# Two reordered edits and one merged instruction in a two-block transformer kernel on one NeuronCore

## The reference, cut to what matters

```
g = sigmoid(gates + gate_bias)                                # three gates of 1024 columns a token
mixed = g[0] * (ya @ w_oa) + g[1] * (yb @ w_ob) + g[2] * (yc @ w_oc)     # the output projections
x = x + mixed @ w_out
x = x + memory_cross_attention(rmsnorm(x), rmsnorm(mem), w_mq, w_mkv, ..., w_mo)
```

## Time and profile before

| | |
|---|---|
| runs | 1175.42 us median of 3 |
| profiled execution | 1174.49 us, span 1172.8 us |
| PE busy | 1143.1 us (97%) |
| DVE busy | 811.8 us (69%) |
| ACT busy | 621.8 us (53%) |
| mean granted TensorE clock | 0.996 |
| DMA | 164 GB/s read over the span; a 1 MB load of `w_up` lands in 5.8 us |

### The profile page before, as it was taken

How to read it: one execution, slowest core, us unless ns; L and a number is a source line. 1 busy time by engine, 2 the same in 40 slices (tenths; PEclk the granted TensorE clock), 3 DMA queues, 4 the chain that set the end, 5 groups by cost and what they waited for, 6 DMA issues and landing times.

```text
span 1172.8 us, 16767 instructions
## 1 busy us (share of the span) xinstructions
PE 1143.1 (97%) x6741; PEld 997.6 (85%) x6741; DVE 811.8 (69%) x884; ACT 621.8 (53%) x808; POOL 81.7 (7%) x114
## 2 busy tenths in 40 slices
PE   8999999899999999999999999999999998999997
PEld 8978888798987799999888888888777887888886
DVE  6897657866878577777548777547866747777743
ACT  7666446436578455555445444436356547444432
POOL 7101100200000000000000000002700000000000
PEclk9999999999999999999999999999999999999999
DMA  8644333324665344645655656565634533666560
GB/s 259 194 153 144 102 108 108 121 96 146 229 199 181 108 162 145 215 155 205 216 179 179 197 181 197 187 205 167 203 117 135 180 108 125 192 204 182 181 212 36
DMA packets 143396, 193.95 MB, mean 165 GB/s; under 512 B 6168, under 2 KB 119192, under 8 KB 143320
## 3 DMA queue, kind: packets, MB, share of 16 engines
q1 hardware_dynamic: 142120, 188.43, 49.6%
q0 software_dynamic: 1200, 4.46, 1.1%
HBM read 191.82 MB, written 1.05 MB: 164 GB/s over the span
## 4 chain that ended last, share of the span: by engine, by line
PE 82%; DVE 10%; ACT 4%; issue 2%; DMA 1%; SPq 0%; DVEq 0%; ACTq 0%
PE banks L1342 22%; PE banks L1376 20%; PE banks L1324 13%; PE banks L1345 11%; PE banks L1361 5%; DVE wlo L1948 4%; PE banks L1352 2%; PE banks L1602 1%; ACT whi L1662 1%; PE banks L1487 1%; PE banks L1390 1%; PE banks L1474 1%; DMA raw<-in_w_in 1%; PE banks L1560 1%; PE banks L1432 0%
## 5 line engine op out<-in xcount | busy, mean ns | idle before, releaser
L1948 DVE TENSOR_TENSOR wlo<-raw,whi 128x2048 fp32r<-128x2048 f32 (+1 forms) x178 | 406.4, 2291 | 124.2 <-ACT whi L1662 124.1
L1662 ACT ACTIVATE whi<-raw 128x2048 fp32r<-128x2048 f32 (+1 forms) x179 | 340.1, 1903 | 246.0 <-PE banks L1345 142.9
L1342 PE MATMUL banks<-xhl,whi 128*128 128x512 f32 x1200 | 384.6, 402 | 2.9 <-DVE y5l L2291 1.8
L1345 PEld LDWEIGHTS banks<-xhl,wlo 128*128 128x128 f32 x1200 | 225.4, 188 | 53.2
L1345 PE MATMUL banks<-xhl,wlo 128*128 128x256 f32 x1200 | 236.3, 278 | 0.0
L1342 PEld LDWEIGHTS banks<-xhl,whi 128*128 128x128 f32 x1200 | 183.9, 189 | 9.5 <-issue 4.6
L1324 PE MATMUL banks<-xhl,whi 128*128 128x256 f32 x912 | 165.5, 284 | 1.1 <-DVE wlo L1948 0.5
L1324 PEld LDWEIGHTS banks<-xhl,whi 128*128 128x128 f32 x912 | 142.0, 192 | 1.9 <-DVE xhl L1975 1.0
L1324 PE MATMUL banks<-xhl,wlo 128*128 128x256 f32 x456 | 129.0, 283 | 0.0
L1376 PE MATMUL banks<-whi,hh 128*128 128x512 f32 x264 | 102.9, 390 | 0.0
L1376 PE MATMUL banks<-wlo,hh 128*128 128x512 f32 x264 | 102.8, 389 | 0.0
(11 more groups left out here) (374 smaller groups left out, 1542.6 us busy)
## 6 DMA issues: line engine op xcount, KB each, us to landing
raw<-in_w_in SPq DMA_DIRECT2D x40, 1024.0 KB, 5.3
raw<-in_w_up SPq DMA_DIRECT2D x22, 1024.0 KB, 5.8
raw<-in_ffn_w_gate SPq DMA_DIRECT2D x22, 1024.0 KB, 5.4
raw<-in_ffn_w_up SPq DMA_DIRECT2D x22, 1024.0 KB, 5.3
raw<-in_ffn_w_down SPq DMA_DIRECT2D x22, 1024.0 KB, 5.0
raw<-in_w_down SPq DMA_DIRECT2D x11, 1024.0 KB, 5.4
raw<-in_w_out SPq DMA_DIRECT2D x8, 1024.0 KB, 5.2
raw<-in_xa_wkv SPq DMA_DIRECT2D x8, 1024.0 KB, 5.5
```

The lines of the kernel that those rows point to most:

```text
L1342: pe.matmul(bank(b[m]), wh[:, k, m * P:(m + 1) * P], both[:, k, :, :].rearrange("p a t -> p (a t)"), start=(k == 0), stop=(k == KD - 1), s ...
L1345: ins = pe.matmul(bank(b[m])[:, 0:T], wl[:, k, m * P:(m + 1) * P], Xh[:, k, :], start=False, stop=(k == KD - 1), skip_group_check=True)
L1662: act.activation(columns(whi, c, part), columns(raw, c, part), ACT.Copy).then_inc(act_done, 1)
L1948: dve.tensor_tensor(columns(wlo, c, part), columns(raw, c, part), columns(whi, c, part), ALU.subtract).then_inc(dve_done, 1)
```

## The change

Three edits. The output projections exchange their bank pairs: i = 0 writes (2, 3), i = 1 writes (0, 1). `g_vb` becomes one `tensor_tensor` over 128 x 512 with beta broadcast along each head's 128 columns, in place of four `tensor_scalar` over 128 x 128. For memory attention alone, the links are cut in another place: lane 0 becomes [sc0 sm0 ex0] [pn0] [pt0 sc2 pc0] [pv0 oc0 ol0 sm2 ex2] [pn2] [pt2 pc2] [pv2 oc2 ol2], and lane 1 likewise. With it, when `mm` has to force links because a step that it needs isn't placed, only chains that still contain such a step are forced; the others are taken if they fit.

```diff
-                            i=i, banks=(2 * i, 2 * i + 1), evac="gated"))
+                            i=i, banks=(2 - 2 * i, 3 - 2 * i), evac="gated"))
...
-    def hook(force=False):
-
-        chosen = [chain for chain in side if chain and (force or fits(chain))]
+    def hook(force=False, until=()):
+
+        chosen = [chain for chain in side if chain and (force or fits(chain) or any(s[1:] in until for link_ in chain for s in link_ if not callable(s)))]
...
         while any(step not in pl.number for step in pl.ready[c]) and side:
-            hook(True)
+            hook(until=[step for step in pl.ready[c] if step not in pl.number])
...
-            if nxt is not None:
+            if nxt is not None and kind in ("mem",):
+                turn_.insert(1, ("pe", "sc", kind, nxt))
+                out_ += [("dve", "sm", kind, nxt), ("act", "ex", kind, nxt)]
+            elif nxt is not None:
                 turn_ = [turn_[0], ("pe", "sc", kind, nxt), turn_[1], ("dve", "sm", kind, nxt), ("act", "ex", kind, nxt)]
                 out_.insert(1, ("dve", "pn", kind, nxt))
             links += [turn_, out_]
+            if nxt is not None and kind in ("mem",):
+                links += [[("dve", "pn", kind, nxt)]]
...
-                for h in range(NH):
-                    ins = dve.tensor_scalar(gVb[:, h, :], bank(5)[:, h * P:(h + 1) * P], gcols[:, t, 0, h:h + 1], None, ALU.mult)
-                ins.then_inc(dve_done, 1)
+                dve.tensor_tensor(gVb[:, :, :], per_head(bank(5)), gcols[:, t, 0, :].unsqueeze(2).to_broadcast([P, NH, P]),
+                                  ALU.mult).then_inc(dve_done, 1)
```

## The result

The changed kernel took 1178.05 us in the median of 7 runs (1176.52 to 1179.02); the kernel before took 1173.95 us beside it (1173.04 to 1175.80). The ratio is 1.0029, with a 95% interval of 1.0017 to 1.0040, some 3.4 us, which is how far the means lie apart (1177.9 and 1174.5); the medians lie 4.1 us apart. Measured a second time the ratio was 1.0026 (1.0016 to 1.0036; medians 1178.06 and 1174.54). So the change makes the kernel slower, by about 0.3%. The forecast was +1.7 us, 1177.1 us. The profiled execution after took 1177.11 us with a span of 1175.4, against 1174.49 and 1172.8: +2.6 us.

A forecast was written before the change was run, and what follows sets the result against it. The prediction took the kernel as a PE stream, busy 97% of the span, with a few gaps. Its terms, -0.84 - 0.43 + 2.95 = +1.7 us, gave 1177.1 us on the median, range 1173.6 to 1179.6.

The forecast's parts named there:

- Part A: Output projection banks: chunk 33 starts 1.47 us sooner, chunk 35 then waits 0.6 us for `gated 33`; -0.84 us kept.
- Part B: Second `g_vb` before `l_u`: one instruction of 687 ns replaces four taking 1.12 us; -0.43 us carried on.
- 0, if that wait grew: Bound on the `g_vb` gain: nothing saved if PE's following 0.88 us wait for ACT's `z_x` grew.
- Part C: Memory attention: `hi 52` behind `ex2` delays chunk 51 by 0.55 us and chunk 52 by 2.95; cost +2.95 us.
- Whether the clock falls during chunk 51 does not matter here: Before chunk 52: PE would be through by 407 either way, and DVE's row sets the end.
- The sum: Whole kernel: -0.84 - 0.43 + 2.95 = +1.7 us, put on the median as 1177.1 us.
- A second fall of the clock: Rival, gaps around `pt3` and `pv3`: clock falls again, costing 1.5 us; total +3.2, 1178.6 us; chance 0.33.
- the main case: Whole kernel: the three edits' terms add to +1.7 us, 1177.1 us, range 1176.2 to 1178.2; chance 0.40.
- The outputs do come early: Rival at chunk 51: `ol1` ends before `pv1`, removing the 2.22 us wait and clock fall; -5.0, 1170.4 us; chance 0.13.
- Part C does nothing: Rival in chunk 51: `pn3` keeps its place, `pt3` and `pv3` stay hidden; -1.3 us, 1174.1 us; chance 0.14.
- adds up for slower: Whole kernel above 1177.8 us: second fall but for a sixth, plus a fifth of the main case; chance 0.37.
- equal gaps need not cost the same: PE clock: the monitor runs on its own phase, so a thin stretch around 406.9 to 410.8 us is at risk.

The follow-up runs named there:

- part C alone: Only the memory attention links and `until` changed, banks and value scaling as in the kernel before; ratio 1.0037 against that kernel.
- e9: The changed kernel itself, all three edits, measured a second time against the kernel before; ratio 1.0026, median 1178.06 us.
- e6: All three edits, and the planner may place a memory attention link 1.0 us ahead of its inputs instead of 0.5; ratio 0.9987 against the kernel before.
- B alone: Only the `g_vb` value scaling made one DVE instruction instead of four, against the kernel before; ratio 0.9998.
- e1: Only the bank pairs of the two output projections swapped, against the kernel before; ratio 0.9996.
- e7: Bank swap and single `g_vb`, old memory attention links, planner allowed 1.0 us ahead of inputs; ratio 0.9984 against the kernel before.
- e8: Bank swap and single `g_vb`, old memory attention links, planner allowed 2.0 us ahead of inputs; ratio 1.0009 against the kernel before.
- e11: Bank swap and single `g_vb`, old links, plus 12 unread transposes filling PE's wait ahead of chunk 51; ratio 0.9987 against the kernel before.
- e4: Bank swap and single `g_vb` together, memory attention as in the kernel before; ratio 0.9988 against that kernel.
- e10: Changed kernel with unread transposes filling PE's waits ahead of chunk 51, `pt3`, `pv3` and chunk 52; ratio 1.0018 against the kernel before, median 1176.14 us.
- e12: Bank swap and single `g_vb`, old links, planner allowed 1.0 us ahead, no transposes, measured again; ratio 0.9983 against the kernel before.

## Why the prediction came out as it did

**Part A: right.** -0.84 forecast, -0.72 kept when alone, and the wait that takes back a part is the one named, 0.71 us for `gated 33` against 0.6 worked out.

**Part B: the size of the step right, the term wrong.** "So each call becomes 0.43 us shorter" holds to 0.01 us, and the 0.88 us wait did not grow, as forecast. What failed is that the gain is carried to the end: of 0.43 some 0.31 to 0.36 is lost at the `hn_mul` of `mk1`, in every profile with part B. The bound "0, if that wait grew" was near the end of it, by another wait than the one named.

**Part C: the mechanism right, the size near.** The order of the three lists is the one worked, step for step, and 2.95 us became 2.7 (2.71 in the first profile of the change, 2.66 in the second, 2.69 alone). "Whether the clock falls during chunk 51 does not matter here" is nearly right. With a fall the two chunks start 11.8 us apart in both profiles of the change, and 11.3 where the clock was held by filling. With part C alone the spacing was 11.8 again without that fall; there the fall at 408.6 us made `pv3` longer (1.60 us against 1.13). In all three the 0.5 us is paid. What the sum left out is the other side: with the old order the fall at 400 us costs the full 1.6 us. Where it did not come (the banks alone), PE was 2.1 us ahead at the start of chunk 52, and 0.5 us ahead at that of chunk 51:

```profile
398.06 0.47 PE L1376 MATMUL banks<-whi,y2h 128*128 128x512 f32 x1 [2.22 <-DVE y2l L2170]
...
405.86 0.40 PE L1376 MATMUL banks<-whi,y2h 128*128 128x512 f32 x1
```

Against such an execution part C costs 1.6 us more. The timed executions at the highest mean clock, 0.998, which spent least time at the low level, go the same way: part C alone took 1176.41 us (one execution) against 1173.0 for before (median of six), 3.4 us. The forecast had taken one profiled execution, with a fall at 400 us, for all of them.

**The sum.** Like for like (e9, equal low stretches) the terms read off PE's distance to before are: PE's start +0.13, part B -0.45, part A -1.62 and +0.80, slower matmuls of the projections +0.51 (below), the `hn_mul` of `mk1` +0.35, part C +2.70, the rest -0.07. That is +2.35 us against +1.7 forecast; the first and the fifth do not belong to the change. Without them it is +1.71, the forecast to 0.01 us, and that is luck: part B came out 0.33 us worse, part C 0.25 better and the rest 0.07 better. The timed +3.1 to +3.4 us is about twice the forecast, and the changed kernel's lower mean clock stands beside it. That 1177.1 us came within 1 us of the median is luck too: it was put on a median of three, 1175.42, and with four more executions that median is 1173.95.

**The cases.** "A second fall of the clock" was given 0.33, with 1.5 us for it. It does occur: at 408.6 us with part C alone, 6.8 us long and worth 2.2 us there. It does not occur in either profile of the changed kernel, both of which had the fall at 398 or 399 first. By their times alone the five executions at 1176.5 to 1176.8 would fit the main case, most of the ten others the second. Where the clock fell in an execution that was only timed is not known, so the share of the second fall in the median stays open; that filling the waits takes some 0.9 us off, with intervals that overlap, is what the runs show of it. "The outputs do come early" would have needed `add 50` ahead of `lo 52` as well as `ol1`, as e6 shows. "Part C does nothing" fell with `pn3`, where the forecast had put the miss. `until` was not tried by itself. (The chances that the forecast adds up for slower make 0.36 and not 0.37.)

The Trainium skill, TensorE: Matmul & The Clock Gate, section Part 1: The HAM clock gate, was cited for a monitor that runs on its own phase, and from that the prediction took that equal gaps need not cost the same. The traces agree that they need not: of the seven profiles with a wait of 2.2 to 2.5 us ahead of chunk 51 (before, the changed kernel twice, A alone, B alone, C alone, A and B) five have a low stretch right behind it and two have none. That the phase is the reason no run here shows.

## What to carry to other kernels

Placing a consumer's step earlier in a list is only worth what its own queue allows: here the outputs went ahead of the next softmax, but `hi 52`, `lo 52` and `add 50`, which the same chunk needs, went behind it. Work the order out for all engines before costing any step; it was exact here, and it named the loss. And when one profile shows a fall of the clock, ask in how many executions it is there: 14 of 30 executions of the kernel before were at a mean clock of 0.997 or more, and none of 15 of the changed one.

## What the runs showed that was not expected

*A fall that stays out can come elsewhere.* Of the eight profiles with no low stretch from 395 to 415 us, five (e1, e6, e7, e8, e11) have one of 3.4 us between 842 and 863 us, where neither the kernel before nor any run with a low stretch at 398 to 409 us has one; e4, e10 and e12 have none in either place. (e8 had one at 390 us as well.)

*The output projections have two speeds at the same granted clock.* Windows of 10 us, the same kernel in two executions (the changed one, first and second time):

```profile
292.00:302.00 10.00, 10.00 (x91) 10.00 (x90) 9.32 (x10) 8.61 (x11) 0.00 (x0) 1.00 0.97 336
```
```profile
292.00:302.00 10.00, 10.00 (x88) 10.00 (x87) 8.92 (x10) 8.20 (x11) 0.00 (x0) 1.00 0.95 339
```

91 matmuls against 88, 113 ns against 118 from one start to the next, with PE busy throughout and the clock at 1.00. Seven of the fourteen profiles were in the slower one. It cost 0.8 to 1.2 us by 310 us, of which later waits took up a part. What sets it is not known; since the same kernel shows both, it is no part of the change.

*A step was 0.35 us late after six instructions had been taken from its engine.* It is the `hn_mul` of `mk1`. The two lines of ACT and DVE before, then after, with the weight load on PE that waits for the `lo` behind that step:

```profile
364.47 0.63 ACT L1771 ACTIVATE PT<-PT 128x512 f32<-128x512 f32 x1
...
365.21 0.75 DVE L2051 SCALAR_TENSOR_TENSOR mk_<-mk_,pcol,PT 128x512 f32<-128x512 f32 x1 [2.44 <-ACT PT L1771]
```
```profile
363.60 0.63 ACT L1776 ACTIVATE PT<-PT 128x512 f32<-128x512 f32 x1
...
364.69 0.75 DVE L2056 SCALAR_TENSOR_TENSOR mk_<-mk_,pcol,PT 128x512 f32<-128x512 f32 x1 [2.79 <-ACT PT L1776]
...
367.69 0.19 PEld L1366 LDWEIGHTS banks<-whi,mhl 128*128 128x128 f32 x1 [0.46 <-DVE wlo L1953]
```

ACT, which the profile names, is not late: the step starts 0.11 us after ACT's end before and 0.46 us after it with the change, so the delay sits on DVE itself. The trace lists transfers of instructions apart from the others. One 8 KB packet of them (q14) came at 360.8 us before; after, it came at 365.4 us, 0.7 us behind the start of the delayed step. The lines of that queue, before from 360 to 362 us, then after from 365 to 367 us:

```profile
q14 instruction: 1, 0.01, 1.9%
```
```profile
q14 instruction: 1, 0.01, 1.5%
```

In either window the other kernel has none. The packet came between 360.6 and 361.2 us in all three profiles without part B, and between 365.3 and 366.7 in all eleven with it. Counted along DVE's records, the packet kept its place: in all fourteen profiles the last record that begins before it is the 449th or 450th, while the steps stand six records earlier with part B. That DVE waited for its own instructions there would fit; it was not tested.
